# A hybrid decoder layer on one core: beta and alpha products made in the first norm, gate sums beside head 0, small loads issued by ScalarE, and all gathers of the last stage queued at once

## What is computed

```python
h = rmsnorm(x, ln1_g)
z = h @ w_in          # q_A | k_A | v_A | qkv_B | beta_B | alpha_B | outgate_B | gate_A | gate_B
# A: dilated sliding-window attention, 3 groups of 8 heads
# B: gated DeltaNet, 8 heads of 128
beta = sigmoid(b_raw)                                   # 8 columns of z
g = -exp(a_log) * softplus(a_raw + dt_bias)             # 8 columns of z
gc = cumsum(g) within a chunk; decay = exp(gc_i - gc_j) # used by every head
x = x + (sigmoid(gate_A) * (o_A @ W_A) + sigmoid(gate_B) * (o_B @ W_B)) @ w_o
# mixture of experts: each token goes to 2 of 32 experts; y rows lie in expert order
x = x + w0 * y[dest0] + w1 * y[dest1]                   # the last stage
```

## Time and profile before

| | us |
|---|---|
| median of 3 runs | 3180.73 (3177.16 to 3184.13) |
| profiled execution, its own time | 3173.9 |
| its span | 3172.2 |

### The profile page before, as it was taken

How to read it: one execution, slowest core, us unless ns; L and a number is a source line. 1 busy time by engine, 2 the same in 40 slices (tenths; PEclk the granted TensorE clock), 3 DMA queues, 4 the chain that set the end, 5 groups by cost and what they waited for, 6 DMA issues and landing times. The chain is left out here.

```text
span 3172.2 us, 33419 instructions
## 1 busy us (share of the span) xinstructions
PE 2852.2 (90%) x12984; PEld 1945.6 (61%) x12984; DVE 897.1 (28%) x1773; ACT 625.5 (20%) x1392; POOL 528.3 (17%) x543
## 2 busy tenths in 40 slices
PE   7999999999379999999999987999999499999992
PEld 4555776776157777777777776888855244444441
DVE  3222222222614334333433432212112411111113
ACT  2111112112013233332322332112000011111110
POOL 3122122222223122222312210000000000000002
PEclk9999999999669999999999969999999699999996
DMA  6002000200701011101100135662031399999994
GB/s 218 11 8 97 14 24 14 74 31 30 250 1 27 1 28 28 28 1 28 28 1 28 28 130 170 207 212 88 21 110 54 146 412 392 382 382 382 386 371 173
DMA packets 161553, 397.80 MB, mean 125 GB/s; under 512 B 10651, under 2 KB 102043, under 8 KB 149087
## 3 DMA queue, kind: packets, MB, share of 16 engines
q1 hardware_dynamic: 151662, 361.58, 31.2%
q0 software_dynamic: 6176, 21.83, 2.0%
q10 hardware_dynamic: 3584, 12.58, 1.0%
HBM read 323.01 MB, written 73.14 MB: 125 GB/s over the span
## 5 line engine op out<-in xcount | busy, mean ns | idle before, releaser
L440 PE MATMUL at_p<-ring,hT 128*128 128x512 f32 x1152 | 532.1, 610 | 1.6 <-PEq L2663 1.6
L981 PE MATMUL dn_p<-hT,ring 128*128 128x344 f32 x1536 | 483.7, 460 | 14.4 <-DVE dn_nq L1376 12.0
L440 PEld LDWEIGHTS at_p<-ring,hT 128*128 128x128 f32 x1152 | 304.2, 273 | 161.1 <-issue 80.8
L981 PEld LDWEIGHTS dn_p<-hT,ring 128*128 128x128 f32 x1536 | 282.3, 193 | 137.2 <-DVE dn_nq L1376 13.5
L1857 PE MATMUL mx_prod<-hT,ring 128*128 128x256 f32 (+1 forms) x1024 | 233.2, 381 | 3.0 <-PEq L2663 3.0
L1857 PEld LDWEIGHTS mx_prod<-hT,ring 128*128 128x128 f32 x1024 | 194.4, 190 | 31.1 <-issue 3.1
L2569 DVE TENSOR_TENSOR ex_hid<-ex_ps_u,ex_gated 128x512 f32<-128x512 f32 (+1 forms) x32 | 22.2, 693 | 507.5 <-PE ex_ps_u L2504 272.8
L1551 POOL TENSOR_TENSOR ring<-ring,dn_level 128x512 f32<-128x512 f32 x96 | 127.1, 1343 | 148.2 <-DVE ring L1395 80.3
L566 DVE COPY oBT<-at_p 128x256 f32<-128x256 f32 (+1 forms) x96 | 52.5, 547 | 299.6 <-PE at_p L490 299.5
L1533 POOL TENSOR_SCALAR ring<-ring,conv_w 128x1024 f32<-128x1024 f32 x24 | 72.0, 2998 | 363.0 <-ACT ring L1200 363.0
L1857 PE MATMUL mx_prod<-oBT,ring 128*128 128x256 f32 (+1 forms) x512 | 118.4, 385 | 12.0 <-DMA ring<-in_w_out_b 12.0
(11 more groups left out here) (427 smaller groups left out, 3953.9 us busy)
## 6 DMA issues: line engine op xcount, KB each, us to landing
ring<-in_w_e_gate SPq DMA_DIRECT2D x32, 2048.0 KB, 12.0
ring<-in_w_e_up SPq DMA_DIRECT2D x32, 2048.0 KB, 15.5
ring<-in_w_e_down SPq DMA_DIRECT2D x32, 2048.0 KB, 14.2
y_scratch<-tails SPq DMA_DIRECT2D x16, 2048.0 KB, 8.2
ring<-in_w_in SPq DMA_DIRECT2D x13, 2048.0 KB, 13.5
ring<-in_w_in SPq DMA_DIRECT2D x32, 512.0 KB, 6.6
ring<-in_cache_swa_kv SPq DMA_DIRECT2D x6, 2048.0 KB, 13.6
mx_w_a<-in_w_out_a SPq DMA_DIRECT2D x32, 256.0 KB, 2.9
```

What stands on the lines that cost most here:

```text
L440: mm = nc.tensor.matmul(bank, perm_tokens(m.hT, g, t, k), weights[:, k, :], start=(k == 0), stop=(k == KD - 1))
L981: mm = nc.tensor.matmul(bankp[j][:, 0:C3], weights[:, k, WPOS[part], :], m.hT[:, k, j * C3:(j + 1) * C3], start=(k == 0), stop=(k == KD - 1))
```

## The change

First, `stage_norm1` makes the beta and alpha products itself. `w_ba` gets a semaphore of its own (`ba_landed`), SyncE issues only `ln1` and `w_ba` ahead of the fifth tile, and ScalarE issues the other ten small loads, two behind each of its first five squares. From the fifth tile's transposes on, TensorE makes the products of earlier tiles between the transposes, and those of the last two tiles at the end. VectorE copies them to `beta_all` and, with `dt_bias` added, to `g_all`.

Second, `stage_deltanet` loses the products and VectorE's copies. ScalarE and VectorE start with the exponentials at once, head 0's projections start at once on TensorE, the sums of g come after slot 6 of head 0 (step 31 of 104), and their exponentials at slot 7 of ScalarE's list. The exponential of `a_log` moves ahead of the logarithm.

Third, `stage_combine` gathers into the weight ring, with a buffer and a semaphore for each tile, so GpSimd waits for nothing; VectorE adds in place into `x1`, which SyncE stores.

```diff
@@ stage_norm1
                     if t == XB:
                         load_small(sp, m, LN1)
-                        for i in range(len(m.small_loads)):
-                            if i != LN1:
-                                load_small(sp, m, i)
+                        load_small(sp, m, BA)
...
+                    for i in others[2 * t:2 * t + 2]:
+                        load_small(act, m, i)
...
+                dve.wait_ge(m.small_landed, 16 * (len(m.small_loads) - 2))
+                dve.wait_ge(ba_done, 1)
+                dve.wait_ge(cleared, 2)
+                for t0, t1, r in ((0, NT, P), (NT, NT + 1, NB)):
+                    nc.vector.tensor_copy(m.beta_all[0:r, t0:t1], ba[0:r, t0:t1, 0:DNH]).then_inc(ba_kept, 1)
+                    nc.vector.tensor_tensor(m.g_all[0:r, t0:t1], ba[0:r, t0:t1, DNH:16],
+                                            bcast(m.dt_bias[0:r].unsqueeze(1), [r, t1 - t0, DNH]), ALU.add
+                                            ).then_inc(ba_kept, 1)
...
+                def gate_products(t, n):
+                    pe.wait_ge(written, t + 1)
+                    for k in range(KD):
+                        mm = nc.tensor.matmul(ba[0:n, t, :], m.hT[:, k, t * P:t * P + n], m.w_ba[:, k, :],
+                                              start=(k == 0), stop=(k == KD - 1))
+                    if t == NT:
+                        mm.then_inc(ba_done, 1)
...
+                    if t == 4:
+                        pe.wait_ge(m.ba_landed, 16)
+                    for u in {4: (0,), 5: (1, 2), 6: (3, 4), 7: (5,), 8: (6,)}.get(t, ()):
+                        gate_products(u, P)
+                for t, n in tiles[NT - 1:]:
+                    gate_products(t, n)
@@ stage_deltanet, TensorE
-                pe.wait_ge(m.small_landed, 16 * (len(m.small_loads) - 1))
-                ba = x[0].rearrange("p c k -> p (c k)")[:, 0:16 * (NT + 1)].rearrange("p (t c) -> p t c", c=16)
-                for t in range(NT + 1):
-                    r = P if t < NT else NB
-                    for k in range(KD):
-                        mm = nc.tensor.matmul(ba[0:r, t, :], m.hT[:, k, t * P:t * P + r], m.w_ba[:, k, :],
-                                              start=(k == 0), stop=(k == KD - 1))
-                mm.then_inc(S["ba_done"], 1)
-                pe.wait_ge(S["g_ready"], 1)
...
+                def gate_sums():
+                    pe.wait_ge(S["g_ready"], 1)
...
+                            if h < 0 and 3 * c + point == 6:
+                                gate_sums()
@@ stage_deltanet, ScalarE
+                            if h < 0 and 3 * c + point == 7:
+                                exponentiate_sums()
@@ stage_combine
+    rows = m.ring.rearrange("p a b -> p (a b)")
+    y = [[rows[:, (2 * t + i) * D:(2 * t + i + 1) * D] for i in range(2)] for t in range(NT + 1)]
...
             for t, r in TILES:
-                    if t >= 2:
-                        pool.wait_ge(both_added, t - 1)
                 for i in range(2):
...
+                nc.vector.scalar_tensor_tensor(x1, y[t][0][0:r], m.row_w[0:r, 0, t:t + 1], x1, ALU.mult, ALU.add
+                                               ).then_inc(first_added, 1)
...
+                sp.dma_start(dst, m.x1[t][0:r]).then_inc(stored, 16)
```

More of the change, by code:

```diff
@@ L51 @@
 RING = 6
-LN1 = 8
+BA, LN1 = 4, 8
 SLOT = KD * 512
@@ L154, in load_small @@
     dst, src = m.small_loads[i]
-    sp.dma_start(dst, src).then_inc(m.ln1_landed if i == LN1 else m.small_landed, 16)
+    sp.dma_start(dst, src).then_inc({LN1: m.ln1_landed, BA: m.ba_landed}.get(i, m.small_landed), 16)
 def build_constants(nc, m, pool):
@@ L227, in build_masks @@
     yield
[L228 removed]
+    pool.wait_ge(m.small_landed, 16 * (len(m.small_loads) - 2))
     step(nc.gpsimd.tensor_scalar(m.qk_gain[:, 0], m.qk_gain[:, 0], float(E) ** -0.5, None, ALU.mult))
@@ L260, in _ @@
                     load_chunk(sp, m, n)
-                sp.wait_ge(m.small_landed, 16 * (len(m.small_loads) - 1))
+                sp.wait_ge(m.small_landed, 16 * (len(m.small_loads) - 2))
             @block.scalar
             def _(act):
+                others = [i for i in range(len(m.small_loads)) if i not in (BA, LN1)]
                 for t, n in tiles:
@@ L1313, in _ @@
                 step = Chain(dve, S["dve_step"])
-                ba = x[0].rearrange("p c k -> p (c k)")[:, 0:16 * (NT + 1)].rearrange("p (t c) -> p t c", c=16)
                 nc.vector.memset(raw[:, 0:3], 0.0).then_inc(S["raw_zero"], 1)
                 step(nc.vector.memset(plus_half, 0.5))
-                step(nc.vector.memset(gate[:, 0:2], 0.0))
-                dve.wait_ge(S["ba_done"], 1)
-                for t0, t1, rows in ((0, NT, P), (NT, NT + 1, NB)):
-                    step(nc.vector.tensor_copy(gate[0:rows, 1, t0:t1], ba[0:rows, t0:t1, 0:DNH]))
-                    step(nc.vector.tensor_tensor(gate[0:rows, 0, t0:t1], ba[0:rows, t0:t1, DNH:16],
-                                                 bcast(m.dt_bias[0:rows].unsqueeze(1), [rows, t1 - t0, DNH]), ALU.add))
-                nc.vector.tensor_copy(gate[:, 5], gate[:, 0]).then_inc(S["gates_stepped"], 1)
                 dve.wait_ge(S["act_gates"], 5)
-                dve.wait_ge(S["gates_stepped"], 1)
                 step(nc.vector.tensor_scalar(gate[:, 1], gate[:, 1], 1.0, None, ALU.add))
                 step(nc.vector.reciprocal(m.beta_all, gate[:, 1]))
-                step(nc.vector.scalar_tensor_tensor(out=gate[:, 5], in0=gate[:, 0], scalar=0.0, in1=gate[:, 4],
+                step(nc.vector.scalar_tensor_tensor(out=gate[:, 5], in0=m.g_all, scalar=0.0, in1=gate[:, 4],
                                                     op0=ALU.max, op1=ALU.add))
@@ new lines, in stage_combine, with _ @@
+    rows = m.ring.rearrange("p a b -> p (a b)")
+    y = [[rows[:, (2 * t + i) * D:(2 * t + i + 1) * D] for i in range(2)] for t in range(NT + 1)]
+    first_added, both_added, stored = (semaphore(nc, m, "cb_" + n) for n in ("first_added", "both_added", "stored"))
+    y_landed = [semaphore(nc, m, f"cb_y_landed{t}") for t in range(NT + 1)]
+    with nc.Block() as block:
+        @block.gpsimd
+        def _(pool):
+            for t, r in TILES:
+                for i in range(2):
+                    nc.gpsimd.indirect_dma_start(y[t][i][0:r], None, m.y_scr,
+                                                 bass.IndirectOffsetOnAxis(m.dest_u[0:r, i, t:t + 1], 0)
+                                                 ).then_inc(y_landed[t], 16)
+        @block.vector
+        def _(dve):
+            for t, r in TILES:
+                x1 = m.x1[t][0:r]
+                dve.wait_ge(y_landed[t], 32)
+                nc.vector.scalar_tensor_tensor(x1, y[t][0][0:r], m.row_w[0:r, 0, t:t + 1], x1, ALU.mult, ALU.add
+                                               ).then_inc(first_added, 1)
+                dve.wait_ge(first_added, t + 1)
+                nc.vector.scalar_tensor_tensor(x1, y[t][1][0:r], m.row_w[0:r, 1, t:t + 1], x1, ALU.mult, ALU.add
+                                               ).then_inc(both_added, 1)
+        @block.sync
+        def _(sp):
+            for t, r in TILES:
+                sp.wait_ge(both_added, t + 1)
+                dst = m.y_prompt[t * P:(t + 1) * P, :] if t < NT else m.y_sample
+                sp.dma_start(dst, m.x1[t][0:r]).then_inc(stored, 16)
+            sp.wait_ge(stored, 16 * (NT + 1))
```

73 lines of the change are left out of this document (23 added, 50 removed).

## The result

The changed kernel takes 3154.65 us (median of 4 runs, 3152.41 to 3155.61) against 3179.75 for the kernel before beside it: a ratio of 0.9919, 95% interval 0.9901 to 0.9936. The forecast was 3159. Its profiled execution has a span of 3150.7 us, 21.5 less than the 3172.2 of before; the sum of the forecast was 21.5 as well. By the medians it is 25.1 us less. Here each execution's span is cut at the same five instructions: the first attention product, the first projection (or product) of the DeltaNet stage, the first product of the decay levels there, the first product of the mix stage, the first gather of the last stage.

A forecast was written before the change was run, and what follows sets the result against it. TensorE, busy 90% of the span, was taken as the bound, so its idle or slow stretches matter. Terms -34 + 20.5 - 8 = -21.5 us took 3173.9 to 3152.4; 6.8 more for the median gave 3159, range 3146 to 3172.

The forecast's parts named there:

- 34 forecast: DeltaNet stage without the beta and alpha products: gain of 34 us, range 31 to 35.
- The removed 35.42 us: DeltaNet's start: time ahead of the first projection, 27.66 us of products included, the last 7 us idle TensorE.
- the cover of silu(k): Head 0: silu(k) done at 30.4 us, TensorE needs it at 30.55; each us missing costs one us.
- a prologue that stalls on the gates: Head 0 of the DeltaNet stage: a stall there on the gates would show the prediction wrong.
- +20.5 forecast: First norm with the products added: 20.5 us longer, at mostly the lower clock.
- The choice between the two levels of the clock: First norm: tiles 5, 6 and first product set at full clock, rest lower; all lower +23.0, all full +11.3.
- The long issue of 3.69 us: First norm: one small load's issue took 3.69 us on SyncE, taken as upper bound for ScalarE.
- the 13.7 of the forecast: First norm: ScalarE's fifth square starts at 13.7 us, the fifth tile's transposes at 16.7.
- The rival of a full clock throughout (+11.3): First norm: products run at full clock between transposes; +11.3 us there, total 3150; chance 0.13.
- that of 374 ns a pass (+49): First norm: weights not loaded ahead, each product pass 374 ns; +49 us there, total 3188; chance 0.04.
- -8 forecast: Last stage: gathers no longer wait for VectorE, pairs and stores at 365 GB/s; 8 us less.
- Whether the stores would lag: Last stage: stores keep their share beside queued gathers, gain 8 us; if they lag, gain 12.

The follow-up runs named there:

- products in decode: Changed kernel with the 144 beta and alpha passes moved from the first norm into decode attention; 3139.37 us, ratio 0.9875.
- gathers alone: Kernel before with only the last stage of the changed one; 3164.85 us, ratio 0.9955.
- loads by SyncE: Changed kernel with SyncE issuing all small loads ahead of the fifth tile, ScalarE none; first norm 58.85 us against 49.08, profiled span 3161.3 us.
- products last: Changed kernel with all nine product sets behind all transposes of the first norm; norm 54.72 us against 49.08, profiled span 3157.2 us.

## Why the prediction was right, and which terms were not

**The DeltaNet stage: 34 forecast, 28.2 measured.** The removed 35.42 us are gone in full. The step that failed is the cover of silu(k), "just enough; each us missing costs one us". Its size was nearly right: silu(k) was done 30.7 us after the first projection (forecast 30.4), since Silu's table load, hidden beside the taps before, now lay behind them; and TensorE came for it at 29.85, 0.7 sooner than thought. By the prediction's own sign, a prologue that stalls on the gates, this part failed in a small way. The price of the missing 0.9 us was not what was thought. From the first projection to the level products the kernel before took 66.69 us, the changed one 73.94, 7.25 more, where 1.5 were forecast: 1.7 up to the key products with the wait in it, 3.1 from there to the next projections at the lower clock, 0.8 in those, and 1.7 in a second fall of the clock behind a 0.31 us wait. With the wait removed the stretch was 67.50 and 67.36, a gain of 34.6 to 34.8. So the mechanism of the 34 was right, and what was mis-sized is the price of 0.9 us of waiting, 4.8 us here instead of one. Over the six executions with this wait it was 3.4 to 4.9, as an estimate: their stretches (70.91 to 74.03), less 1.7 where the clock fell behind the 0.31 us wait and 1.4 where the first passes were slow (products in decode), against 67.4. The 1.7 in this execution are no part of the mechanism; the same fall is seen with the old code in gathers alone (6.59 us, 4.89 in the kernel before).

**The first norm: +20.5 forecast, +16.8 measured.** The choice between the two levels of the clock was right: full until 21.85, then 0.50 to the end, as the earlier back-to-back passes had suggested. By that choice the norm was to end near 51.5, and VectorE's last sum ended at 47.5. The 4 us: 0.5 because the fifth tile came at 16.22, not 16.7; 1.7 because the full clock reached into the second pair of sets (32 passes in 5.18, not 6.85); about 1.4 because instructions that follow each other overlap by 0.2 us each in the rows, which adding up durations left out; and 0.4 in VectorE's adds. The long issue of 3.69 us did appear on ScalarE's queue (2.54 us at 6.10), and cost little: the fourth tile's transposes began at 14.19, and at 14.02 in the kernel whose ScalarE issues no loads (loads by SyncE). The fifth square began at 11.77, 1.9 us earlier than the 13.7 of the forecast, but only 0.5 of that reached TensorE, because GpSimd was building masks and took up that tile's sum only behind them, a wait that the prediction doesn't have:

```profile
13.67 0.78 POOL L217 TENSOR_TENSOR mask_pair<-oBT 128x128 bf16<-128x128 f32 x1
...
14.53 0.19 POOL L286 TENSOR_SCALAR n_ssq<-n_ssq 128x1 f32<-128x1 f32 x1
```

In the kernel before, the fifth tile's load stood behind twelve small loads, not eleven; the sum doesn't change by it.

The rival of a full clock throughout (+11.3) and that of 374 ns a pass (+49) are both out.

The Trainium skill, TensorE: Matmul & The Clock Gate, Part 4: PE-mode transpose, says that transposes do not bring the full clock. The trace of the kernel before doesn't agree: the clock rose from 0.50 to 1.00 with nothing but transposes running. In the changed kernel it stood at 0.99 from 16.20 to 21.85, where only transposes had run ahead; with the loads by SyncE, where transposes and product sets follow each other from 21.20 on, it stayed at 0.50.

**The last stage: -8 forecast, -11.1 measured.** The eighth pair landed 32.3 us after the first gather's issue. The prediction names 33 for this, but its own working gives 35.5 (3156.1 less 3120.55), so it was 3.3 us earlier than worked out. The term that was mis-sized is the rate: 365 GB/s was the row of before taken for gathers and stores together, with two pairs queued, and with all queued it was 414 to 419. After the first pair the other seven took 3.67 us each, in steps of 2.8 to 4.6, instead of 4.16. The tail, 8.25 us from the eighth pair to the end, was as forecast (8.3). Whether the stores would lag was the open choice, and they did not: from the last store's issue to the end of the span are 3.12 us, 3.07 before.

**The sum.** The three errors, -3.7 in the norm, +5.8 in the DeltaNet stage, -3.1 in the last, with +1.0 in the attentions, cancel. The +1.0 is within what the same code did from one execution to another there (866.2 to 869.0). So the profiled execution came out at the 3152.4 forecast for it (3152.41). The median was forecast 6.8 us above that, as in the kernel before, and lay 2.2 above it; that is the whole of the difference between 3159 and 3154.65.

**The signs named ahead.** First projection at the stage's first instruction: seen. Product passes of about 0.2 us at 0.50, norm's end between 42 and 58: seen. Gathers without waits for VectorE: seen. No long wait for silu(k): the wait was 0.91 us, short, and what went with it was not cheap.

## What to carry to other kernels

Work that an engine must do is worth moving only into a stretch in which that engine waits for another: the same 144 passes cost 19 us in the norm and, beside VectorE's work in decode attention, no more than that stretch varies by itself. When a cover comes out within a microsecond, move the hidden step earlier rather than count on it: in the six executions in which TensorE waited 0.9 us at the key products, 3.4 to 4.9 us went in all, most of it at the lower clock. For transfers, first read how many of them are queued when the engines show gaps; a buffer for each tile brings nothing if a wait still holds the queue at two.

## What the runs showed of the hardware that was not expected

- Behind waits of 0.91 and 0.28 us in an otherwise dense stretch the granted clock fell to 1.2 GHz in six executions out of six (mean of 10 us 0.66 or 0.83); in five executions without a wait there it stayed at 2.4 GHz. Behind one wait of 0.31 us it fell in some executions (1.7 us lost) and not in others with the same code, and behind one of 0.55 us in the changed kernel it did not.
- Passes of 16 columns kept the full clock for 2.6 us (products last) to 4.6 us (changed kernel, with one tile's transposes among them) when it was granted already, and did not raise it: 35.8 us of transposes and such passes without a gap stayed at 0.50.
- Gathers and stores together moved 369 GB/s at first and then 414 to 422 with all pairs queued, 354 to 409 with three, and 167 to 366 in turns with two (stretches of 6 us).
